# Six norms with a filling chunk: the first two blocks of the new activations turned in one batch behind the third block of the last chunk

## What is computed

```python
for layer in range(DEPTH):
    h = rmsnorm(x, norm_w[layer, 0])
    x = x + 0.5 * swiglu(h, gate, up, down)              # d_ff = 2816
    h = rmsnorm(x, norm_w[layer, 1])
    x = x + (even_mixer(h, ...) if layer % 2 == 0 else odd_mixer(h, ...))
    h = rmsnorm(x, norm_w[layer, 2])
    x = x + cross_attention(h, memn, wq, wkv, wo)
    h = rmsnorm(x, norm_w[layer, 3])
    x = x + 0.5 * swiglu(h, gate, up, down)
return rmsnorm(x, final_norm_w)
```

## Time and profile before

| | us |
|---|---|
| median of 3 runs (1201.43 to 1202.47) | 1201.73 |
| the profiled execution, its own time | 1201.93 |
| span of the profiled execution | 1200.0 |
| PE busy, PE weight loads busy | 1191.0, 1045.8 |
| DVE busy, ACT busy, POOL busy | 793.0, 642.0, 121.8 |
| share of the chain that ended last on PE | 95% |

### The profile page before, as it was taken

The page is one execution under the profiler, slowest core; times in us unless marked ns, Lnnn a source line. Parts: engine busy times, 40 slices in busy tenths (PEclk is TensorE's granted clock), DMA queues, the critical chain, the costliest instruction groups (busy, mean ns, idle before and its releaser), DMA issues.

```text
span 1200.0 us, 17666 instructions
## 1 busy us (share of the span) xinstructions
PE 1191.0 (99%) x7001; PEld 1045.8 (87%) x7001; DVE 793.0 (66%) x841; ACT 642.0 (53%) x871; POOL 121.8 (10%) x105
## 2 busy tenths in 40 slices
PE   9999999999999999999999999999999999999997
PEld 8888889889989888888888888899988898888886
DVE  6766766865657676656676656677786676666664
ACT  7554546553556554444465444454676565544443
POOL 1000001640142020000020000020012122000001
PEclk9999999999999999999999999999999999999999
DMA  9966655544444465656556556555623425665560
GB/s 319 338 206 187 199 179 172 164 157 142 140 157 156 141 211 185 200 177 205 177 175 194 191 183 202 178 162 187 211 102 110 147 100 176 228 192 193 182 203 35
DMA packets 164880, 214.75 MB, mean 179 GB/s; under 512 B 14816, under 2 KB 140896, under 8 KB 164704
## 3 DMA queue, kind: packets, MB, share of 16 engines
q1 hardware_dynamic: 164544, 213.30, 54.7%
q0 software_dynamic: 144, 0.52, 0.1%
q10 hardware_dynamic: 144, 0.26, 0.1%
HBM read 213.02 MB, written 1.05 MB: 178 GB/s over the span
## 4 chain that ended last, share of the span: by engine, by line
PE 95%; DMA 2%; DVE 1%; ACT 1%; issue 0%; POOL 0%; SPq 0%; POOLq 0%; DVEq 0%
PE ps L2012 29%; PE ps L1991 15%; PE ps L2019 15%; PE ps L1992 15%; PE ps L1993 15%; PE ps L2076 1%; DMA raw<-in_ffn_w_down 1%; DMA raw<-in_first_up 1%; ACT xn L1175 1%; PE ps L2531 0%; PE ps L2620 0%; PE ps L2658 0%; PE ps L2681 0%; PE ps L2287 0%; PE ps L2139 0%
## 5 line engine op out<-in xcount | busy, mean ns | idle before, releaser
L2012 PE MATMUL ps<-hT,w_hi 128*128 128x512 f32 x1568 | 374.8, 391 | 0.7 <-DVE hT L1283 0.5
L2012 PEld LDWEIGHTS ps<-hT,w_hi 128*128 128x128 f32 x1568 | 289.9, 188 | 58.8 <-DVE hT L1283 0.7
L1398 DVE TENSOR_TENSOR w_lo<-raw,w_hi 128x2048 fp32r<-128x2048 f32 x108 | 247.6, 2292 | 61.5 <-ACT w_hi L831 61.5
L1243 DVE TENSOR_TENSOR w_lo<-raw,w_hi 128x2048 fp32r<-128x2048 f32 x85 | 195.2, 2306 | 72.3 <-ACT w_hi L701 72.3
L701 ACT ACTIVATE w_hi<-raw 128x2048 fp32r<-128x2048 f32 x85 | 162.2, 1914 | 87.3 <-PE ps L1993 85.8
L2019 PEld LDWEIGHTS ps<-hT,w_lo 128*128 128x128 f32 x1568 | 201.5, 191 | 8.0
L831 ACT ACTIVATE w_hi<-raw 128x2048 fp32r<-128x2048 f32 x108 | 205.8, 1906 | 0.5 <-DMA raw<-in_ffn_w_gate 0.5
L2019 PE MATMUL ps<-hT,w_lo 128*128 128x256 f32 x1568 | 204.0, 283 | 0.0
L1991 PE MATMUL ps<-w_hi,arena_r 128*128 128x512 f32 x354 | 138.4, 391 | 0.2 <-DVE arena_r L1391 0.2
L1992 PE MATMUL ps<-w_lo,arena_r 128*128 128x512 f32 x354 | 137.8, 389 | 0.0
L1993 PE MATMUL ps<-w_hi,arena_r 128*128 128x512 f32 x354 | 137.4, 388 | 0.0
(11 more groups left out here) (320 smaller groups left out, 1629.9 us busy)
## 6 DMA issues: line engine op xcount, KB each, us to landing
raw<-in_ffn_w_down SPq DMA_DIRECT2D x44, 1024.0 KB, 4.8
raw<-in_ffn_w_gate SPq DMA_DIRECT2D x43, 1024.0 KB, 5.3
raw<-in_ffn_w_up SPq DMA_DIRECT2D x43, 1024.0 KB, 5.3
raw<-in_xattn_wkv SPq DMA_DIRECT2D x16, 1024.0 KB, 5.5
raw<-in_even_w_in SPq DMA_DIRECT2D x13, 1024.0 KB, 5.1
raw<-in_xattn_wq SPq DMA_DIRECT2D x8, 1024.0 KB, 5.2
raw<-in_xattn_wo SPq DMA_DIRECT2D x8, 1024.0 KB, 4.9
raw<-in_odd_w_in SPq DMA_DIRECT2D x6, 1024.0 KB, 5.7
```

The source lines that it names most:

```text
L1243: ins = V.tensor_tensor(lo, src, hi.bitcast(F32), ALU.subtract)
L1398: V.tensor_tensor(w_lo[:, m % RING, :], raw[:, m % RING, :], w_hi[:, m % RING, :].bitcast(F32), ALU.subtract).then_inc(lo_done, 1)
L2012: mm(ps[:, bank0 + m, :], cols(w_hi, n, k, CW, m * P, (m + 1) * P), hT[:, k, :, :].rearrange("p a c -> p (a c)"), start=k == 0, stop=False)
```

## The change

For the keys in `FILL`, `turn_ahead` turns nothing behind block 1, and both first blocks, eight transposes, behind block 2. For the seventh norm all stays as it was.

```diff
             def turn_ahead(v, key):
 
                 def between(i):
-                    if i:
+                    if key in FILL:
+                        if i == 2:
+                            transposes(x_ready(v, key), x, turn_order(key)[:2], key)
+                    elif i:
                         transposes(x_ready(v, key), x, turn_order(key)[i - 1:i], key)
                 return between
```

## The result

The changed kernel takes 1209.82 us (median of 6 runs, 1209.79 to 1210.18), the kernel before 1201.66 us (median of 6 runs, 1201.43 to 1202.47) beside it. That is 8.2 us more; the ratio is 1.0067, with a 95% interval of 1.0057 to 1.0078. Forecast were 1210.0 us, and 8.3 us more than before. The profiled execution took 1209.81 us, with a span of 1207.9.

What follows compares the result with a forecast made beforehand. PE was taken to bound the kernel, 95% of a 1200.0 us span. 6 x (1.36 + 0.02) = 8.3 us on 1201.93 gives 1210.2, forecast as 1210.0 us because the median is 0.2 lower; range 1206.5 to 1213.0.

Steps and rivals of the forecast that it cites:

- the chain from the first transposes to the third add: First norm: PE transposes of (0,0), ACT, DVE low parts, third add, PE load of block (1,0)'s transposes; 3.65 us.
- The head moves by 1.36 us: Six matmuls of block (1,0) now precede the first transposes, which start at 188.38 instead of 187.02, with 0.05 us slack.
- Rival E: Kernel gets faster: eight transposes in a row save 0.2 to 0.7 us over six places, 1201.0 to 1201.5 us; chance 0.03.
- rival B: ACT gets the first block only behind all eight transposes, or DVE and ACT slow each other: 1212.6 us; chance 0.06.
- PE through at 190.64 to 190.68: First norm: PE finishes both transpose batches and block (1,1) then, at best 0.04 us earlier than before.
- What the profile would show: PE's transposes wait on the third add six times, 1.4 us each, some 8.3 us and more in all.
- The unseen cost of a PE that has run empty: PE restarting after each of six stalls: taken as 0.02 us per place, from a range of 0 to 0.23.
- Nothing given back, nothing late next: Everything behind the third batch comes 1.36 us later; the last turned block keeps 1.8 us of room to its reader.
- rival C: PE's later small waits shrink: 7.5 us remain, or 4.2 us (1206 us) if the stall is also half hidden; chance 0.06.
- The clock costs nothing: At the six stalls of 1.4 us PE's clock stays up, since it fell only after some 2.3 us idle.
- rival D: The clock falls at each of six places, 2 us each: 20.3 us more, 1222 us; chance 0.03.

Runs made afterwards that it cites:

- experiment 6: Changed kernel with the eight joined transposes one block later, behind the fourth block, right ahead of those of block (1,0): 1224.05 us against 1201.80 before the change.
- experiment 4: Changed kernel with nothing joined: transposes of block (0,0) stay behind block (1,0), those of (0,1) go behind block (1,1); 1209.87 us against 1201.76 before the change.
- experiment 5: Changed kernel with transposes of block (0,0) in the middle of block (1,0), those of (0,1) behind it: 1205.74 us against 1201.76 before the change.
- experiment 7: Changed kernel with the eight joined transposes moved to the middle of block (1,1): 1216.40 us against 1201.76 before the change.
- experiment 1: Changed kernel with DVE's third add moved ahead of the low parts of the first turned block: 1201.52 us against 1201.80 before the change.

## Why the prediction was right

**That the chain from the first transposes to the third add sets the third batch**: shown. It is 3.65 us before, after, and in experiment 6, and 3.64 to 3.66 in experiments 4, 5 and 7. The links hold one by one as well. Put 0.32 us later, where the kernel before has its first place, the rows after read 188.38 for the first transposes, 189.02 for ACT, 190.20 for the low parts, 191.24 for the third add and 192.03 for the load; forecast were 188.38, 189.02, 190.19, 191.24 and 192.03. Taking one link out of it, the add's place behind the low parts, takes the whole cost out (experiment 1).

**The head moves by 1.36 us, and there is no slack**: shown by size. 0.68 us of delay at six places cost 4.0 us, 1.36 us cost 8.2 at six and 4.2 at three. (Rival E called the 0.05 us between the add's end and the load slack. They are a link of the chain, and a delay does not eat into them.) ACT's start 0.64 behind the first transposes holds as well (188.70 - 188.06), so `transposed` is in fact seen behind the fourth of eight; rival B is out.

**PE through at 190.64 to 190.68**: the distance from the joined batch to the end of the next block was forecast as 2.26 to 2.30 us, and is 2.25 in experiment 1. The some 0.04 us that joining saves are there in the rows, and are too small to be told in the time.

**What the profile would show**: six waits on this add, right. Their size was given as 1.4 us each and 8.3 in all, and no view shows that: for the matmuls it is 1.24 and 7.2, for the weight loads 1.66 and 9.8. The forecast set a loss of time equal to an idle time, and the two differ by the overlap of the records (above).

**The unseen cost of a PE that has run empty**: taken as 0.02 us from a range of 0 to 0.23. The load and the matmul of the third batch begin at 191.71 and 191.72, as close as before, so it is 0.01 or nothing; the upper end was far off. 6 x 0.02 is the 0.1 us between the forecast's 8.3 and the measured 8.2.

**Nothing given back, nothing late next**: each place costs its full 1.33 to 1.42 us, and from the sixth, late by 7.84, to the end of the span, late by 7.9, nothing comes back. Of the small later waits that rival C counted, 0.3 + 0.3 + 0.2, only the last is gone, 0.16 us at 1010 us, and it does not show in the span. The last turned block of the first norm is ready at 197.03 (195.90 + 1.13) and its reader starts at 198.84, 1.81 us of room as before.

```profile
195.90 1.13 DVE L1275 SCALAR_TENSOR_TENSOR hT<-ps,norm_cols,hT 128x128 fp32r<-128x128 f32 x4 [1.19 <-ACT hT L729]
...
198.84 2.02 PE L2142 MATMUL ps<-hT,small_parts 128*128 128x512 f32 x8
```

**The clock costs nothing**: right for the changed kernel, in which it is 1.00 at the stalls, but on a reason that was too strong, and so in part by luck. I read from the end of the kernel before that the clock held for 2.3 us of idleness, and took this as the room that a stall of 1.4 us has. Experiment 7 shows falls behind stalls of 1.9 us. The 2.3 us were one draw among several: at the end of the changed kernel PE is idle from 1201.6, and the clock falls only after 1206, some 4.6 us later, and at the end of experiment 4 it falls after some 1.9.

```profile
1201.00:1202.00 1.00, 0.58 (x5) 0.38 (x4) 0.96 (x2) 1.00 (x3) 0.82 (x2) 1.00 0.00 0
...
1205.00:1206.00 1.00, 0.00 (x0) 0.00 (x0) 0.00 (x0) 0.00 (x0) 0.00 (x0) 1.00 1.02 375
1206.00:1207.00 1.00, 0.00 (x0) 0.00 (x0) 0.00 (x0) 0.00 (x0) 0.00 (x0) 0.60 1.00 369
```

A fall, where there was one, cost some 1.5 us and not the 2 of rival D. The page "TensorE: Matmul & The Clock Gate" of the Trainium skill says in Part 4 that transposes do not count as busy in the same way. By that rule the prediction added 0.9 us of transposes to the stall, but in PE's order the six matmuls of block (1,1) stand between the two. The eight joined transposes, with these six and then 1.24 us of stall behind them, brought no fall; nor did twelve, with twelve short matmuls and then 0.3 to 0.8 us of stall behind them. Whether those ahead of the longer stalls had a part in the falls no run here tells.

## What to carry to other kernels

Before you move an instruction back on the busiest engine, follow what waits for it round through the other engines to where it comes back to that engine, and add up that chain: if the engine fills it exactly, each microsecond of delay is one of time. An in-order queue makes such chains where there is no dependence: here an add that needed only PE's block stood behind four instructions that needed the transposes. A stall can be taken out at either end, by moving the late instruction up in its queue or by placing independent work ahead of the one that waits.

## What the runs showed of the hardware that was not expected

The clock of TensorE fell in the middle of the kernel behind stalls of 1.9 us, at two of six like places in one profiled run, and behind 2.6 us at four of six; behind 1.24 us it did not fall in the profiled run, and the 6 runs are within 0.4 us, all with a mean granted clock of 0.998 or 0.999. In all six falls of the two profiles PE had already begun again: at the first place of experiment 6 it begins at 193.42, and the window from 193 is still at 0.91. Behind a kernel's last matmul the idleness before the fall was no fixed time either: 1.9 us in experiment 4, 2.3 before the change, 4.6 after it. A fall cost some 1.5 us, with matmuls of 256 columns every 0.21 us in place of 0.12. Like stalls brought a fall and did not, and the time of such a kernel scatters: 3.2 us between four runs in experiment 7. That the falls make this scatter fits their price, but is not shown run by run.
